# Fillers in TensorE's waits, halves of FFN 1's last output pass, and feature-first gemms in a two-block network on one core

## What is computed

```python
def first_block(x, c, ctx, c_ctx, w_mod, b_mod, ...):
    mod_lat, mod_ctx = silu(c) @ w_mod + b_mod, silu(c_ctx) @ w_mod + b_mod     # 9 rows of 1024 each
    x  = x  + 0.5 * ml[2] * swiglu(modulate(rms_norm(x,  norm1_g), ml[0], ml[1]), ffn1_w_in, ffn1_w_out)
    cx = cx + 0.5 * mc[2] * swiglu(modulate(rms_norm(cx, norm1_g), mc[0], mc[1]), ffn1_w_in, ffn1_w_out)
    hx = modulate(rms_norm(x,  norm2_g), ml[3], ml[4])      # norm 2, latents
    hc = modulate(rms_norm(cx, norm2_g), mc[3], mc[4])      # norm 2, context: only its k and v are used
    ...                                                      # q, k, v with norms of q and k; conv; attention
    x = x + ml[5] * merge_branches(...)                      # "res"
    x = x + 0.5 * ml[8] * swiglu(modulate(rms_norm(x, norm3_g), ml[6], ml[7]), ffn2_w_in, ffn2_w_out)
    return rms_norm(x, final_g)

def even_layer(x, ...):      # odd_layer likewise
    h = rmsnorm(x, pre_g)
    ...
    return x + rmsnorm(y @ w_out, post_g)
```

## Time and profile before

| | us |
|---|---|
| runs | 1451.61, 1449.18, 1445.44 |
| profiled execution, time | 1445.66 |
| its span, first to last instruction | 1443.9 |
| TensorE busy | 1350.8 (94%) |
| VectorE busy | 916.1 (63%) |
| ScalarE busy | 647.1 (45%) |
| TensorE's clock, mean granted | 0.979 |

### The profile page before, as it was taken

The page is one execution under the profiler, slowest core; times in us unless marked ns, Lnnn a source line. Parts: engine busy times, 40 slices in busy tenths (PEclk is TensorE's granted clock), DMA queues, the critical chain, the costliest instruction groups (busy, mean ns, idle before and its releaser), DMA issues.

```text
span 1443.9 us, 22946 instructions
## 1 busy us (share of the span) xinstructions
PE 1350.8 (94%) x9170; PEld 1217.2 (84%) x9170; DVE 916.1 (63%) x1459; ACT 647.1 (45%) x1011; POOL 26.0 (2%) x29
## 2 busy tenths in 40 slices
PE   5899999999997999999989999889899999889996
PEld 4478888888876789999989999779888998889996
DVE  2745546655357368777876656588776665487864
ACT  3332221222235244455454445565565775455553
POOL 0000000000010000000000000100000000100001
PEclk9999999999998999999999999999999999999998
DMA  6635334454362234357657755546255454536561
GB/s 243 207 121 174 106 128 160 161 175 133 104 201 89 88 118 146 117 195 243 216 171 256 248 190 183 154 131 192 81 159 160 143 156 130 165 112 190 181 197 37
DMA packets 201402, 229.65 MB, mean 159 GB/s; under 512 B 7120, under 2 KB 191696, under 8 KB 201296
## 3 DMA queue, kind: packets, MB, share of 16 engines
q1 hardware_dynamic: 201008, 227.90, 48.9%
q10 hardware_dynamic: 288, 0.29, 0.1%
HBM read 227.11 MB, written 1.05 MB: 158 GB/s over the span
## 4 chain that ended last, share of the span: by engine, by line
PE 56%; DVE 7%; ACT 3%; DMA 2%; issue 2%; POOL 0%; SPq 0%; ACTq 0%; DVEq 0%; POOLq 0%
PE P L823 15%; PE P L824 15%; PE P L825 15%; DMA W<-in_ffn_w_in 2%; PE P L829 1%; PE P L830 1%; PE P L831 1%; DVE WL L1548 1%; ACT WH L1204 1%; PE P L922 1%; PE P L910 1%; DVE TS L1399 1%; DVE RS L1630 1%; PE P L899 1%; DVE XL L1409 1%
## 5 line engine op out<-in xcount | busy, mean ns | idle before, releaser
L1548 DVE TENSOR_TENSOR WL<-W,WH 128x1024 fp32r<-128x1024 f32 x358 | 431.2, 1217 | 318.1 <-ACT WH L1204 317.2
L823 PE MATMUL P<-XH,WH 128*128 128x256 f32 (+1 forms) x1808 | 563.5, 312 | 24.0 <-DVE XL L1409 11.9
L824 PE MATMUL P<-XL,WH 128*128 128x256 f32 (+1 forms) x1808 | 549.7, 304 | 0.0
L825 PE MATMUL P<-XH,WL 128*128 128x256 f32 (+1 forms) x1808 | 549.2, 304 | 0.0
L1204 ACT ACTIVATE WH<-W 128x1024 fp32r<-128x1024 f32 x358 | 368.3, 1042 | 254.6 <-PE P L825 135.8
L823 PEld LDWEIGHTS P<-XH,WH 128*128 128x128 f32 x1808 | 344.8, 191 | 52.7 <-issue 21.0
L824 PEld LDWEIGHTS P<-XL,WH 128*128 128x128 f32 x1808 | 344.8, 191 | 20.1 <-issue 2.9
L825 PEld LDWEIGHTS P<-XH,WL 128*128 128x128 f32 x1808 | 344.2, 190 | 17.2
L823 PE MATMUL P<-GH,WH 128*128 128x512 f32 (+1 forms) x352 | 119.9, 341 | 0.3 <-DVE WL L1548 0.3
L825 PE MATMUL P<-GH,WL 128*128 128x512 f32 (+1 forms) x352 | 119.0, 338 | 0.0
L824 PE MATMUL P<-GL,WH 128*128 128x512 f32 (+1 forms) x352 | 119.0, 338 | 0.0
(11 more groups left out here) (280 smaller groups left out, 1804.7 us busy)
## 6 DMA issues: line engine op xcount, KB each, us to landing
W<-in_ffn_w_in SPq DMA_DIRECT2D x88, 512.0 KB, 5.3
W<-in_w_in_ab SPq DMA_DIRECT2D x72, 512.0 KB, 3.5
W<-in_w_modt SPq DMA_DIRECT2D x64, 512.0 KB, 3.9
W<-in_w_in SPq DMA_DIRECT2D x52, 512.0 KB, 4.2
W<-in_ffn_w_out SPq DMA_DIRECT2D x40, 512.0 KB, 4.9
W<-in_w_in_c SPq DMA_DIRECT2D x32, 512.0 KB, 4.4
W<-in_w_out_ab SPq DMA_DIRECT2D x16, 512.0 KB, 3.4
W<-in_w_out_c SPq DMA_DIRECT2D x16, 512.0 KB, 3.5
```

The lines of the kernel that those rows point to most:

```text
L823: pe.matmul(o, h[:, k, c], xh[:, kk, a:b], start=kk == 0, stop=False)
L824: pe.matmul(o, h[:, k, c], xl[:, kk, a:b], start=False, stop=False)
L825: mm = pe.matmul(o, l[:, k, c], xh[:, kk, a:b], start=False, stop=kk == gm.nk - 1)
L1548: dve.tensor_tensor(l, a, h.bitcast(F32), ALU.subtract).then_inc(S["wl"], 1)
```

## The change

- **Fillers.** `warm(n, bank)` issues n products of the ones block with the first 256 columns of the constants into a bank that the next gemm will overwrite; nobody reads them. Nine stand ahead of everything, behind the constants' load. At norms 3, 4 and 5 three follow the last `ones`, then TensorE waits for the root, then four more. At post-norm 0 the same seven, and one behind each of six `ones` of norm 5.
- **Roots' table.** A root of one column (`root_table`) is put on ScalarE where the fifth feature's square is due, in the last pass ahead of norms 2 to 4 and both post-norms.
- **Opening.** The broadcast and its copy become a step r2. Order: s1 0, s1 1, r1 0, r2 0, r1 1, shifts 0, r2 1.
- **Feature-first.** A `first` gemm takes both tiles for each k, instead of all k of a chunk for tile 0 and then for tile 1. The ones products of a last gemm stand behind each tile's end as before.
- **Halves.** The gemm m = 6 of FFN 1's last pass runs its three chunks for the latents' 256 columns, then again for the context's. The latents' squares and ones products (step os 0) come after the first context chunk; reciprocal (oi), features 0 to 3 (nr) and one split come before the third; features 4 to 7 and a split behind it. The context's ones products (os 1) come after the first q gemm, its reciprocal and features 0 to 3 after the second, 4 to 7 after the third.

The diff, cut; the parts of ScalarE and VectorE for norms 3 to 5 keep what they did.

```diff
@@ -303,11 +303,13 @@
             scales(k)
         self.step("s1", a=1)
         self.step("r1", a=0)
+        self.step("r2", a=0)
         self.step("r1", a=1)
         self.up("sq", 8)
         self.up("on", 2)
         self.nb_free = self.up("sr")
         b = shifts(0)
+        self.step("r2", a=1)
         split(0)
         self.step("mt", a=0, bank=b)
@@ -335,12 +337,63 @@
         self.part(gb, 4, chunks[3])
         self.split_to(n + LOOK)
 
+    def halves(self, wt, r0, nk, c0):
+
+        parts, k = [], 0
+        while k < nk:
+            m = min(4, nk - k)
+            src = wt[r0 + k * 128:r0 + (k + m) * 128, c0:c0 + 256].rearrange("(t p) c -> p t c", p=128)
+            parts.append((k, m, self.chunk(src, m)))
+            k += m
+
+        def run():
+            self.step("scales", a=1, b=4)
+            n = self.chunks[parts[-1][2]][0]
+            for v, cols in ((0, (256, 512)), (1, (0, 256))):
+                gm = Gemm("fx1", 6, 12, wt, r0, nk, c0, cols, True, False)
+                base = len(self.tile_end)
+                gm.tiles = [base, base + 1]
+                for _ in gm.tiles:
+                    self.tile_end.append(0)
+                    self.tile_free.append(self.up("xu1"))
+                for i, (k0, m, j) in enumerate(parts):
+                    last = k0 + m == nk
+                    if v == 0:
+                        self.split_to(n + 1)
+                    elif i == 2:
+                        self.step("oi", a=0, b=self.roots["n2", 0])
+                        self.step("nr", a=0, b=0)
+                        self.split_to(n + 2)
+                    for t in gm.tiles if last else (0,):
+                        self.marks += 1
+                        if last:
+                            self.tile_end[t] = self.marks
+                    self.chunk_end[j] = self.marks
+                    self.step("ck", gemm=gm, k0=k0, nk=m, chunk=j, a=int(last))
+                    if v == 1 and i == 0:
+                        self.root("n2", 0)
+                        self.step("os", a=0)
+            self.step("nr", a=0, b=4)
+            self.split_to(n + 3)
+        self.prog.append(run)
+
+    def context_norm(self, i):
+        if i == 1:
+            self.step("oi", a=1, b=self.roots["n2", 1])
+        self.step("nr", a=1, b=4 * i - 4)
+
+    def root(self, *name):
+
+        self.nb_free = self.up("sr")
+        self.roots[name] = self.nb_free[1]
+        return self.nb_free[1]
...
@@ -378,12 +431,16 @@
 
         self.mod_list([2, 3, 4, 5])
         self.ffn(1, w["ffn1_w_in"], w["ffn1_w_out"], ALL)
-        self.call(self.norm, 2, 1, 4)
 
 
         WIN = w["w_in"]
         for i in range(4):
             self.gemm("q", i, WIN, 0, 8, 3072 + 256 * i, LAT, first=i == 0)
+            if i == 0:
+                self.call(self.root, "n2", 1)
+                self.call(lambda: self.step("os", a=1))
+            elif i < 3:
+                self.call(self.context_norm, i)
             if i % 2:
                 self.call(lambda i=i: self.back.append(self.qk_norm(i // 2)))
@@ -472,15 +529,18 @@
     def norm(self, n, scale=0, row=0):
         if scale:
             self.step("scales", a=scale, b=row)
-        self.nb_free = ("two", 1) if n == 4 else self.up("sr")
-        self.step("norm", a=n)
+        if n == 4:
+            self.nb_free = ("two", 1)
+        else:
+            self.root("n", n)
+        self.step("norm", a=n, b=len(self.tile_end) % 4)
 
     def post(self, i):
         self.ended(f"p{i}")
-        self.nb_free = self.up("sr")
+        self.root("post", i)
         if i == 0:
             self.stats("s6", False)
-        self.step("post", a=i)
+        self.step("post", a=i, b=len(self.tile_end) % 4)
@@ -506,6 +566,9 @@
                 self.call(self.ended, "hx", n)
                 self.call(self.stats, "s2" if n == 1 else "s4")
             for m in range(0, 8, 2):
+                if n == 1 and f0 == 12 and m == 6:
+                    self.halves(wout, f0 * 128, f1 - f0, m * 128)
+                    continue
                 self.gemm(f"fx{n}", m, wout, f0 * 128, f1 - f0, m * 128, (0, b - a), g=f0, first=m == 0,
                           norm=f0 == 12 and m == 6)
@@ -798,45 +861,53 @@
                     xh, xl = MOVING.get(kind, (XH, XL))
                 _, h, l = parts(s.chunk)
                 pe.wait_ge(S["wl"], s.chunk + 1)
-                for j, t in enumerate(gm.tiles):
+                order = [(j, k) for j in range(len(gm.tiles)) for k in range(s.nk)]
+                if gm.first:
+                    order.sort(key=lambda o: o[1])
+                for j, k in order:
+                    t, kk = gm.tiles[j], s.k0 + k
                     ps = P[:, t % 4, :]
-                    if s.k0 == 0 and t >= 4:
+                    if kk == 0 and t >= 4:
                         name, v = plan.tile_free[t - 4]
                         pe.wait_ge(S[name], v)
...
+                    if kk == gm.nk - 1 and kind in SUMS and (kind[:2] != "fx" or gm.g == 12):
                         m = gm.i + j if kind[:2] == "fx" else 2 * gm.i + j
                         if m >= 6:
                             ones(SUMS[kind], m - 6)
 
-            n_at = 0
+            def warm(n, bank=3):
+
+                for _ in range(n):
+                    pe.matmul(P[:, bank, 0:256], con("one"), C[:, 0:256], start=True, stop=True)
+
+            pe.wait_ge(SI[1], 16)
+            warm(9)
             for s in seq:
...
+                elif s.kind == "os":
+                    sq0, pa0, on0, nb = stat["s2"]
+                    c = slice(256 - 256 * s.a, 512 - 256 * s.a)
+                    for i, slot in enumerate((0, 2, 1)):
+                        if i:
+                            pe.wait_ge(S["sq"], sq0 + 6 + 2 * s.a + i)
+                        else:
+                            pe.wait_ge(S["pa"], pa0 + 5)
+                            pe.wait_ge(S[nb[0]], nb[1])
+                        pe.matmul(NB[:, c], con("one"), SQ[:, slot, c], start=i == 0, stop=i == 2).then_inc(S["on"], 1)
...
@@ -881,11 +962,21 @@
                             ones(name, i)
                     else:
                         ones(name, 2)
+                    warm(3, s.b)
+                    if s.a == 4:
+                        pe.wait_ge(S["tw"], 2)
+                    else:
+                        pe.wait_ge(S["sr"], plan.roots["n", s.a])
+                    warm(4, s.b)
                 elif s.kind == "post":
                     ones("s5" if s.a == 0 else "s7", 2)
                     if s.a == 0:
+                        warm(3, s.b)
+                        pe.wait_ge(S["sr"], plan.roots["post", 0])
+                        warm(4, s.b)
                         for i in range(6):
                             ones("s6", i)
+                            warm(1, s.b)
                 elif s.kind == "qa":
@@ -1051,6 +1142,11 @@
                     c += n
                 sq.then_inc(S["sq"], 1)
 
+            def root_table(i):
+
+                act.wait_ge(S["sc"], 1)
+                act.activation(SC[:, i:i + 1], con("eps"), ACT.Sqrt)
+
             def high(n, k, q, cols, shift):
 
@@ -1086,9 +1182,18 @@
                     elif kind[:2] == "fx":
                         if g == 12:
                             k = i + j
-                            act.wait_ge(S["xu" + kind[2]], 8 + k + 1)
+                            act.wait_ge(S["xu" + kind[2]], 8 + k + 1 + (2 if kind == "fx1" and k >= 6 and gm.cols[0] == 0 else 0))
+                            if k == 4:
+                                root_table(int(kind[2]))
                             if kind == "fx1":
-                                square("s2", k, (X[:, k, :], 1.0))
+                                if k < 6:
+                                    square("s2", k, (X[:, k, :], 1.0))
+                                else:
+                                    a = gm.cols[0]
+                                    if a:
+                                        act.wait_ge(S["pa"], stat["s2"][1] + k - 2)
+                                    act.activation(SQ[:, 8 - k, a:a + T], X[:, k, a:a + T], ACT.Square) \
+                                        .then_inc(S["sq"], 1)
                             else:
                                 square("s4", k, (X[:, k, 256:512], 1.0), (X[:, k, 256:512], vec("fin", k)))
@@ -1119,6 +1224,8 @@
                         act.wait_ge(S["g"], end["mc"])
                         act.activation(YH[:, k, :], X[:, k, 0:T], ACT.Copy, scale=0.5).then_inc(S["o2h"], 1)
                     elif kind == "res":
+                        if k == 4:
+                            root_table(3)
                         act.wait_ge(S["rse"], k + 1)
                         square("s3", k, (X[:, k, 256:512], 1.0))
...
                             act.wait_ge(S["k3"], 2 * (m - 2) + 2)
                         act.activation(E["z"][:, m % 2, j, :], ps, ACT.Tanh, scale=0.5).then_inc(S["szt"], 1)
```

(31 more changed lines are left out.)

119 lines of the change are left out of this document (56 added, 63 removed).

## The result

The changed kernel took 1424.54 us in the median of four runs (1423.11 to 1427.31) beside 1447.36 for the kernel before: a ratio of 0.9841, 95% interval 0.981 to 0.9871. A second set of five runs beside another eleven of the kernel before gave 1427.48 against 1446.44, 0.9864 (0.9843 to 0.9884). So the change saves 19 to 23 us; I forecast 15.9. Its profiled execution took 1427.31, the slowest of the first four, with a span of 1425.5, 18.4 under the 1443.9 of before.

What follows compares the result with a forecast made beforehand. TensorE, busy 94% of the span, bounds the kernel, so only its idle and slow time can give. Terms 7.5 + 3.9 + 0.9 + 0.1 + 0.5 + 2.1 + 0.9 = 15.9 us, hence 1433 for the median; range 1421 to 1442.

Steps and rivals of the forecast that it cites:

- third rival: Fills hold the clock at norms 2, 3 and 5: three half-clock stretches, 1.0 each, giving 1430; chance 0.10.
- second rival: Opening: fillers hold the clock through the 64 one-column products, at half their 0.218; 7.0 more, 1426; chance 0.08.
- (a): Opening: second broadcast moves behind the first shift product, which starts at 28.57; net 2.4 us earlier.
- (b): Opening, chunk of k 0 to 3: feature-first runs two features of both tiles before the third arrives; saves 1.3.
- (c): Opening, chunk of k 4 to 7: feature-first shrinks the 1.9 wait and the clock should stay; saves 3.1.
- (d): Opening: nine fillers after the constants land, until about 11.7, may lift the clock; 0.7, from 0 to 7.7.
- Norm 2: Between FFN 1 and the k pass: halves remove the gap before q, later waits take some back; 3.9 saved.
- Norm 3: Before FFN 2: earlier root table, feature-first gemm and fillers, one half-clock stretch instead of two; 0.9 (0.5 to 2).
- Post-norm and norm 5: Before the odd layer: earlier root table 0.9, first gemm 1.2 more; 2.1 in all (0.9 to 3).
- first rival: Norm 2 pays in full, the q-norm wait staying near 1.6: 5.8 more, 1427; chance 0.15.
- the sixth: Slower: context's norm stands before q and k norms on ScalarE and VectorE; 1452 with 24 us of waits; chance 0.02.
- the fourth: The opening gives half, its freed time caught by the next weights: 11 in all, 1438; chance 0.09.

Runs made afterwards that it cites:

- e7: Changed kernel with the opening's second broadcast again ahead of the first shift product; 1429.86 us against 1447.63, ratio 0.9877.
- e5: Changed kernel with the first gemms back in tile order, the sort by k left out; 1434.85 us against 1447.63, ratio 0.9915.
- the second profile: Nothing changed: the changed kernel profiled again in its second set of runs, that set's slowest; 1434.01 us.
- e1: Changed kernel without any fillers, all calls of `warm` left out; 1436.3 us against 1447.0, ratio 0.9918.
- e3: Changed kernel with the norms' fillers 128 columns wide instead of 256; 1427.41 us against 1447.0, ratio 0.9863.
- e6: Changed kernel without the early loads of the root table (`root_table` left out); 1430.8 us against 1447.63, ratio 0.9884.
- e10: Changed kernel plus context norm in pieces, fillers among the context's one-column products and for every other TensorE wait over 1.4 us; 1418.67 us, ratio 0.9803.
- e8: Changed kernel with norm 2 whole: FFN 1's last pass over 512 columns, both norm parts behind it, no fillers there; 1431.52 us, ratio 0.9899.
- e13: e10 with fillers behind three groups of the latents' and two of the context's one-column products, instead of three context groups; 1417.3 us, ratio 0.9801.
- e2: Changed kernel with only the opening's nine fillers, those of the norms left out; 1433.89 us against 1447.0, ratio 0.9904.
- e9: Changed kernel plus one filler behind each of the first three groups of the context's one-column products; 1430.82 us against 1446.44, ratio 0.9892.

## Why the prediction was right or wrong

The direction, the size to 7 us and most mechanisms were right: 15.9 forecast, 18.4 by the two profiles and 19 to 23 by the runs. The third rival came true for norms 3 and 5, though not at its price of 1.0 each. The second came true in part: one of my own signs of being wrong, one-column products in half their time, holds for the first 32 of the 64. Some of the sum's nearness is luck: the opening's fillers gave more than I had, norm 2 in the profiles less.

**(a) Second broadcast, 2.4.** Right: without fillers the shift product starts at 28.54 (I had 28.57), and the first split at 34.26 against 36.71 before, 2.45 earlier. Undone with the fillers in place (e7) it costs 2.2 beside the execution whose clock fell as early.

**(b) Chunk of k 0 to 3, 1.3.** Right in kind, too large, and dependent on the clock. The idle time in the chunk is gone (0.6 before and in e5, none in the changed kernel), and with one half-clock stretch in it the chunk takes 7.4 instead of 8.3. The chunk stands behind the 3.4 wait for ScalarE's copy, and where two stretches follow that wait it takes 8.3 again (the second profile, e1, e3 and e6): "Saves 1.3" had the clock as given. With that wait filled (e10) it takes 6.2.

**(c) Chunk of k 4 to 7, 3.1.** Right: from the start of one chunk to that of the next 67.66 to 77.47 became 61.72 to 68.43, 3.1 less, without the stretch at half clock, and tile order brings 9.65 back.

**(d) Nine fillers, 0.7.** Mis-sized: 2.6, and 0.8 to 4.4 by the execution (experiment 1). They last 6.59, not some 4 (18 records: one product stands as two, and takes 0.46 at the full clock, which I had at the half one), so the one-column products follow without the idle 2 us that I had, and the first 32 run at 0.11 each. That is the second rival's mechanism; it gave 2.6 of its 7.0, since the context's squares do not come before 18 (TensorE waits 0.40 for them) and the clock fell at 19.4.

**Norm 2, 3.9.** Each step is there: q starts 1.84 behind the reciprocal's end with no gap, 3.06 idle ahead of the fifth feature (3.2), 6.39 ahead of the q norm (6.1), half clock behind both. The stage gave 2.6 and -0.8 in two profiles, and 4.9 by the medians (e8). Mis-sized by the clock terms: I had 0.8 for a half-clock stretch, and in the first profile 3.44 us of work stood at half clock behind the fifth feature and 3.66 around the wait of 6.4, so some 1.7 and 1.8 (estimates: half of each). The second profile had one stretch more. My bound of 9.7, what the norm gives before the context's steps, is near what e10 reached with the pieces and the fillers together: 476.88 - 467.41 = 9.5.

**Norm 3, 0.9.** Wrong in size: the stage gained 3.7 to 4.7, and not for the reason of the third rival, since without any filler and with two half-clock stretches it gained 4.2 all the same. The norm's reciprocal parts it in two. From there on the changed kernel gained 2.0 and 3.1 (79.8 before, 77.9 and 76.7 in its two profiles), and e1 2.7. The fillers are seen in the first 48 products, 7.0 instead of 7.7 before and 8.1 in e1, and in the first profile still at the 192nd, 23.5 against 24.4 in e1; behind it the waits for weights took this 1.0 back. TensorE waited for WL 2.0 us from 735 to 815 there and 0.7 in e1 (the second profile had 1.0, and kept more of the gain):

```profile
PE P L888 <- DVE WL L1667: 2.0, 3, 0.9
```
```profile
PE P L888 <- DVE WL L1665: 0.7, 2, 0.4
```

"Past that the weights' loads set the pace and take some back" fits that. What else there is stands one step earlier: 1.7 of the 3.7 came ahead of the reciprocal, 0.5 of them by the root's table as I had it. For the rest, TensorE waits ahead of the norm for GpSimd's sum of the first six squares in the kernels whose stage is long, and (0.2 or less) not in the changed one or e1. Before and e13 (127.47):

```profile
PE P L789 <- POOL SQ L1024: 0.8, 1, 0.8
```
```profile
PE P L856 <- POOL SQ L1132: 2.0, 1, 2.0
```

It is 0.8 in e5, 1.5 in e8 and 0.9 in e10. By these traces the sum is late where a weight load is. ScalarE's split of a chunk of w_out, 14 us ahead of the reciprocal, waits for its landing; VectorE's updates stand in the queue behind that chunk's low half, and the squares behind the updates. In the changed kernel and in e13:

```profile
709.27 1.06 ACT L1313 ACTIVATE WH<-W 128x1024 fp32r<-128x1024 f32 x1 [0.40 <-DMA W<-in_w_out]
```
```profile
705.34 1.06 ACT L1330 ACTIVATE WH<-W 128x1024 fp32r<-128x1024 f32 x1 [1.47 <-DMA W<-in_w_out]
```

That wait is 1.4 to 2.3 in the five kernels with the late sum (before, e5, e8, e10, e13) and at most 0.6 in the nine other profiles; the load took 5.4 to 6.3 us to land in the five and 4.4 to 4.7 in the others. My sum had no term for it. Why the load is slower in some stays open. e2's 127.57 has no such wait; 1.4 of what it is longer came ahead of the reciprocal too, with a wait of TensorE of 1.6 for weights earlier in the stage.
*My prediction held a rule of the Trainium skill, "TensorE: Matmul & The Clock Gate", section "What's actually happening", against the 1.9 gap of before: a filled gap would not fall. By that rule, the traces agree: e10 fills all but a few waits (up to 2.0 are left), and up to the last matmul nothing behind the opening falls. With the openings they do not agree: in e5 and e13 the clock fell with TensorE busy throughout.*

**Norm 4, 0.1:** 0.0, at any clock. **Even layer's output pass, 0.5:** not seen apart from the heads. **Post-norm and norm 5, 2.1:** the stage gave 1.6, but both steps are there in full. The root's table gave 0.9 (VectorE's wait for the root was 3.48 before, 2.60 after, 3.48 again in e6). The first gemm's 48 products took 5.8 instead of 7.5, where I had 5.9 on the full clock, and 8.0 without fillers (e1). e3, e7 and e8 keep all of that (73.0, 2.6 less than before); the changed kernel's two profiles are 1.0 longer behind these products, for a reason that I can't name. **End, 0.9:** 0.9.

**Costs elsewhere, nothing:** right for the fillers behind waits; among the one-column products (e9) they stood in the way. The fillers together are worth 10 of the 21 (e1); my sum had 0.7 for the opening's, and at norms 3 and 5 one half-clock stretch less, some 0.8 each.

The first rival (norm 2 in full) and the sixth (slower) did not come; the fourth (half the opening) neither: 8.9 against 7.5, 7.5 again in the second profile; nor the fifth (5 left).

## What to carry to other kernels

Where TensorE idles for a known wait, unread products in that wait cost nothing that shows here and mostly kept the clock. Waits of 1.8 us were followed by a half-clock stretch in some executions and not in others, so filling the short ones too (e10, e13) gave 7 to 8 us more than the changed kernel, some of it by the pieces of the context's norm. Cut the steps of a norm that is not needed yet into pieces between chunks, because in a FIFO engine they stand ahead of small steps that TensorE needs next. Read the granted clock of several executions beside every profile before a difference of a few us is explained.
